# State-space segments from ten-row products of cumulative sums, in a two-block fp32 kernel on one core

## The chip, the cores and the metric

The kernel runs on one core of one Trainium2 chip. The metric is the device time of one execution in microseconds (us), as the median of several; a lower number is better. The engines of the core are named as in the profile: PE is the matrix engine (PEld its weight loads), DVE the vector engine, ACT the scalar engine, POOL the GpSimd engine, SP the engine that issues most transfers.

## The reference

A sequence of 512 tokens of width 1024 goes through a first block (gated convolution, feed-forward, banded attention, feed-forward) and a second block (a state-space mixer, "SSD", then gated linear attention, "GLA"), all in fp32. The part that the change touches is the scan of the SSD mixer, which is run forwards and, on the reversed sequence, backwards; `cum` is the running sum of the negative log decays `lac` within a chunk of 128 tokens:

```
cum = jnp.cumsum(lac, axis=1)
decay = jnp.exp(jnp.where(causal, cum[:, :, None] - cum[:, None], -jnp.inf))
xdt = xc * dtc[..., None]
cb = jnp.einsum('blgn,bsgn->blsg', cc, bc)
y = jnp.einsum('blsgr,bsgrp->blgrp', cb[..., None] * decay, xdt)
y = y + jnp.einsum('blgn,bgrpn->blgrp', cc, state) * jnp.exp(cum)[..., None]
```

`dt` is a softplus of a projection to 2 x 32 heads plus a bias, and `lac = dt * a`. There are 8 groups of 4 heads, and 4 chunks.

## The kernel before

Every engine has its own program, written out by hand in program order; semaphores named with `S(...)` tie them together. Nothing is reordered by a scheduler. The weights come in 168 units of 1 MB: SP loads a unit (`load`), ACT rounds it to `whi` (`high`), POOL makes the rest `wlo` (`low`), and PE computes each product as three matmuls, hi x hi, hi x lo and lo x hi (`product`, L1684 to L1686). The normed input is kept as `hHi`, `hLo` in the fixed part of SBUF. Everything else that a stage needs lies in areas that are laid over one another, behind the fixed tiles; the last fixed tiles are `stat`, `g45` (8 columns of 4 bytes) and the two `t32`. The moving operands of the output projections (`yHi`, `f0aHi`, `f1aHi`, `oHi`, `sHi`, `gHi` and their low parts) are in such areas.

The SSD stage first projects x, B, C and `dt` of group 0, turns `dt` into log decays `la` per token, and makes `ecum`, `wst` and `etot` with 24 small matmuls against triangles of ones (L2010). Then it runs `group(g)` for 8 groups. On PE a group is: `turn_in` (transposes and B C^T), `segments` for 4 chunks, the projections of group g+1 (`project(g + 1, q)`, q = 0 to 3) put between them, `turn_out` of the group before, `increments` of the states, `chunk_out` for 4 chunks, and the two halves of z (`z_half`). The work on a chunk n = 4g + c is:

- ACT builds eight 128x128 pieces `Rm` (mask times a log decay, `segment_rows`, L854), PE multiplies them by GT and LT, forwards and backwards added in one of two PSUM banks (`seg_bank`, L2049, plain fp32), and ACT takes the exponential there (`exponential`, L859);
- POOL makes `coupling(n)`, decay-free weights times dt (`coupled`, L558 and L561), after the six `xw` products and four `ybuf` products of the group;
- DVE multiplies both into `MT` (`mix`, L1430, semaphore `mt_ready`), which `chunk_out` uses (L2097).

On DVE a group also has `taps` (convolution of the next group's projections, L1396 to L1401), `states` (L1439, L1442), `collect` (the output, L1455 to L1459), `masks`, `normalise` and `gate`. In group 0 DVE scales `xT` in eight operations. After the last group, `chan` over 16 tiles of `sHi`, `sLo` starts the output projection.

## Time and profile before

| | us |
|---|---|
| median of 3 runs (2251.29 to 2252.07) | 2251.39 |
| the profiled execution | 2251.21 |
| its span, first to last instruction | 2249.5 |
| PE busy in it | 2154.9 |
| DVE busy | 978.4 |
| POOL busy | 910.0 |
| ACT busy | 828.5 |

The execution lasts 1.7 us longer than its span. A busy engine is one with an instruction in flight; PE is busy in 96% of the span, with a mean granted clock of 0.976 of its full speed, so what is worth time is what PE does, and where it waits.

### The profile page before, as it was taken

The numbers are of one execution on the slowest core, as the hardware profiler recorded it, in microseconds if no ns is written. First come the engines' busy times: TensorE is split into PE (matmuls) and PEld (weight loads), VectorE is DVE, ScalarE is ACT, GpSimd is POOL, SyncE is SP. The second block draws the span as 40 slices with busy tenths as digits, with TensorE's granted clock in tenths as the row PEclk, the third lists the DMA queues.
The fourth block names the chain that finished last, engine by engine and source line by source line (L and its number), as shares of the span: only waits on it lengthen the run. The fifth ranks groups of instructions, "written<-read, shape, count | busy, mean of one in ns | idle before, by whom it ended". The sixth has DMA issues, their size and how long they took to land.

```text
span 2249.5 us, 27332 instructions
## 1 busy us (share of the span) xinstructions
PE 2154.9 (96%) x10885; PEld 1746.7 (78%) x10885; DVE 978.4 (43%) x1435; ACT 828.5 (37%) x1312; POOL 910.0 (40%) x359
## 2 busy tenths in 40 slices
PE   7999999999999989999999999999989989999898
PEld 5877888888777778888888778888868776866676
DVE  3184533323334345343332776766661244452321
ACT  3123222222444332222232555555562154353342
POOL 3434444444322234443441666666654331221232
PEclk9999999999999999999997999999989999999999
DMA  4223333233332123333332211121113321111221
GB/s 135 95 92 104 94 95 111 77 90 101 117 94 76 57 75 94 94 94 94 92 96 63 57 57 57 57 75 57 57 38 94 97 76 38 57 57 38 57 75 57
DMA packets 233244, 176.55 MB, mean 78 GB/s; under 512 B 8483, under 2 KB 229975, under 8 KB 233128
## 3 DMA queue, kind: packets, MB, share of 16 engines
q1 hardware_dynamic: 230460, 174.29, 25.7%
q8 instruction: 84, 1.38, 0.3%
q10 hardware_dynamic: 2668, 0.63, 0.1%
q14 instruction: 32, 0.26, 0.0%
HBM read 172.75 MB, written 2.14 MB: 78 GB/s over the span
## 4 chain that ended last, share of the span: by engine, by line
PE 57%; issue 30%; POOL 8%; DVE 3%; ACT 2%; POOLq 0%; DMA 0%; ACTq 0%; DVEq 0%
PE bank L1684 16%; PE bank L1686 15%; PE bank L1685 15%; POOL wlo L538 7%; PE bank L2049 2%; PE bank L2246 1%; PE bank L2228 1%; PE bank L2097 1%; PE bank L2093 1%; PE bank L2242 1%; PE bank L2063 1%; PE bank L2210 0%; PE bank L2028 0%; PE bank L2254 0%; POOL P L561 0%
## 5 line engine op out<-in xcount | busy, mean ns | idle before, releaser
L538 POOL TENSOR_TENSOR wlo<-raw,whi 128x2048 fp32r<-128x2048 f32 (+1 forms) x168 | 737.9, 4392 | 1236.9 <-ACT whi L616 1236.9
L1684 PE MATMUL bank<-hHi,whi 128*128 128x512 f32 x1408 | 563.1, 400 | 8.0 <-DVE hLo L1156 5.3
L1686 PE MATMUL bank<-hHi,wlo 128*128 128x512 f32 x1408 | 549.9, 391 | 0.0
L1685 PE MATMUL bank<-hLo,whi 128*128 128x512 f32 x1408 | 549.5, 390 | 0.0
L616 ACT ACTIVATE whi<-raw 128x2048 fp32r<-128x2048 f32 (+1 forms) x168 | 303.8, 1809 | 476.0 <-PE bank L1686 474.3
L1684 PEld LDWEIGHTS bank<-hHi,whi 128*128 128x128 f32 x1408 | 265.3, 188 | 73.8 <-issue 13.7
L1685 PEld LDWEIGHTS bank<-hLo,whi 128*128 128x128 f32 x1408 | 265.4, 188 | 59.8 <-issue 5.7
L1686 PEld LDWEIGHTS bank<-hHi,wlo 128*128 128x128 f32 x1408 | 265.1, 188 | 56.3
L1684 PE MATMUL bank<-whi,hHi 128*128 128x256 f32 x896 | 260.2, 290 | 5.9 <-ACT lg L1026 3.9
L1685 PE MATMUL bank<-wlo,hHi 128*128 128x256 f32 x896 | 255.9, 286 | 0.0
L1686 PE MATMUL bank<-whi,hLo 128*128 128x256 f32 x896 | 255.6, 285 | 0.0
L1684 PEld LDWEIGHTS bank<-whi,hHi 128*128 128x128 f32 x896 | 174.2, 194 | 24.6 <-issue 18.7
L1685 PEld LDWEIGHTS bank<-wlo,hHi 128*128 128x128 f32 x896 | 174.3, 195 | 0.4 <-issue 0.2
L1686 PEld LDWEIGHTS bank<-whi,hLo 128*128 128x128 f32 x896 | 174.3, 195 | 0.0
L1188 DVE TENSOR_TENSOR xT<-xT,bank 128x512 f32<-128x512 f32 x48 | 33.0, 687 | 312.2 <-PE bank L1686 312.2
L636 ACT ACTIVATE hHi<-xT,vecT 128x512 fp32r<-128x512 f32 x40 | 28.0, 717 | 127.0 <-DVE xT L1188 127.0
L1156 DVE SCALAR_TENSOR_TENSOR hLo<-xT,vecT,hHi 128x512 fp32r<-128x512 f32 x40 | 61.2, 1544 | 29.7 <-ACT hHi L636 29.7
L1401 DVE SCALAR_TENSOR_TENSOR xc<-bank,vecT,xc 128x510 f32<-128x510 f32 (+1 forms) x96 | 71.9, 749 | 3.4
L1684 PE MATMUL bank<-f0aHi,whi 128*128 128x512 f32 x176 | 69.5, 395 | 0.0
L1684 PE MATMUL bank<-f1aHi,whi 128*128 128x512 f32 x176 | 69.5, 395 | 0.0
L1686 PE MATMUL bank<-f0aHi,wlo 128*128 128x512 f32 x176 | 69.5, 395 | 0.0
L1686 PE MATMUL bank<-f1aHi,wlo 128*128 128x512 f32 x176 | 69.5, 395 | 0.0
(325 smaller groups left out, 3178.8 us busy)
## 6 DMA issues: line engine op xcount, KB each, us to landing
raw<-in_ssd_w_in SPq DMA_DIRECT2D x48, 512.0 KB, 4.6
raw<-in_ffn_w_gate SPq DMA_DIRECT2D x44, 512.0 KB, 4.7
raw<-in_ffn_w_up SPq DMA_DIRECT2D x44, 512.0 KB, 4.7
raw<-in_gla_w_in SPq DMA_DIRECT2D x40, 512.0 KB, 4.7
raw<-in_conv_w_in SPq DMA_DIRECT2D x24, 512.0 KB, 4.4
raw<-in_ffn_w_down SPq DMA_DIRECT2D x32, 384.0 KB, 3.6
raw<-in_attn_w_qkv SPq DMA_DIRECT2D x24, 512.0 KB, 4.7
raw<-in_ffn_w_down SPq DMA_DIRECT2D x32, 320.0 KB, 4.0
```

Of the source, the lines that this page charges most:

```text
L538: pool.tensor_tensor(wlo[s][:, 0:w], raw[s][:, 0:w], whi[s][:, 0:w].bitcast(F32), ALU.subtract).then_inc(w_lo, 1)
L616: act.activation(whi[s][:, 0:w], raw[s][:, 0:w], ACT.Copy).then_inc(w_hi, 1)
L636: act.activation(dst, src, ACT.Copy, scale=scale).then_inc(sem, 1)
L1156: stt3(tile(hLo, k), tile(xT, k), gain(j, k), tile(hHi, k).bitcast(F32), ALU.mult, ALU.subtract).then_inc(h_ready, 1)
L1188: tt(x, x, bank[b][:, :], ALU.add).then_inc(res_done, 1)
L1401: ins = stt3(y[:, to:to + w], u[:, frm:frm + w], tapcol(j, ct), y[:, to:to + w], ALU.mult, ALU.add)
L1684: pe.matmul(dst, hi1, hi2, start=first, stop=False)
L1685: pe.matmul(dst, hi1, lo2, start=False, stop=False)
L1686: return pe.matmul(dst, lo1, hi2, start=False, stop=last)
L2049: ins = pe.matmul(seg_bank(c)[:, :], mat[:, :], rows(n, d), start=(d == 0), stop=(d == 1))
L2063: ins = pe.matmul(bank[4 + step][:, 256 * d:256 * d + 256], bt[:, P * c:P * (c + 1)], xw_buf(step, d), start=True, stop=True)
L2093: pe.matmul(carried_bank(c, d), conv_tile(g, 3)[:, P * c:P * (c + 1)], m["stt"][:, SEQ * step + 256 * d:SEQ * step + 256 * d + 256], start ...
```

## The change

1. **Segments.** The log decays are not multiplied by triangles any more. `dt` is projected with the 64 heads as rows and the 512 tokens as columns (24 matmuls in place of 96), and DVE runs a scan along the tokens for each direction. The cumulative sums go, split into a high and a low part, to DRAM (`cums`), and 12 small transfers a group bring them back as two operands for each direction: `U` and `L`, ten rows for each chunk (two rows of sums or ones, eight of picks). PE then forms `cum - cum` for 4 heads as one product of ten rows in the faster fp32r format, forwards in bank 2 (`FB`) and backwards in bank 3 (`BB`). ACT copies `BB` to `back` (`back_out`), DVE takes the smaller of both (`least`), ACT the exponential, DVE `mix`. The two banks serve every chunk.
2. **ecum, wst, etot** are made in the same layout and turned to tokens by 12 transposes and one small matmul.
3. **Order.** `mix(n)` of a group's first chunk stands ahead of `taps(g + 1, 0)`; `chunk_out(g, 0)` stands ahead of `segments(g, 3)`; both z halves of group 0 and `project(1, 0)` stand ahead of group 0; the scaling of `xT` is spread over seven groups.
4. **The end.** Part of the splits of `sY` stand inside the last group, and the first output tile is computed over 14 tiles, then the last two.
5. **Areas.** `g45` gets 64 columns, so all areas behind it start 224 bytes later, on the same remainder modulo 512 bytes as `hHi`. With 8 columns they started 288 bytes past it.

```diff
-        m_g45 = sb("g45", [P, KT])
+        m_g45 = sb("g45", [P, 64])
...
+                def decay_rows(g):
+                    if g:
+                        sp.wait_ge(S("rows_ready"), 4 * g)
+                    for d in range(2):
...
+                        for r in range(2):
...
+                            sp.dma_start(U[r::32, :].rearrange("c (h e) -> c h e", h=HPG), src).then_inc(S("rows_in"), 16)
+                        for c in range(NT):
...
+                            sp.dma_start(L[32 * c + 2:32 * c + 2 + 2 * HPG, :], src).then_inc(S("rows_in"), 16)
...
-                def segment_rows(n):
...
-                            act.activation(rows(n, d)[:, P * h:P * (h + 1)], mask[:, :], ACT.Copy, scale=m["la"][:, at:at + 1]).then_inc(S("rm_ready"), 1)
+                def rows(g):
+                    act.wait_ge(S("rows_in"), 192 * (g + 1))
+                    for d in range(2):
+                        for name in (f"U{d}", f"L{d}"):
+                            copy(m[name][:, :], m[f"{name[0]}in{d}"][:, :], S("rows_ready"))
+                def back_out(n):
+                    act.wait_ge(S("seg"), n + 1)
+                    if n:
+                        act.wait_ge(S("seg_least"), n)
+                    if n >= NT and n % NT == 0:
+                        act.wait_ge(S("y_squared"), n)
+                    copy(m["back"][:, :], BB[:, :], S("back_ready"))
                 def exponential(n):
-                    act.wait_ge(S("seg"), n + 1)
-                    act.activation(seg_bank(n)[:, :], seg_bank(n)[:, :], ACT.Exp).then_inc(S("ex_ready"), 1)
+                    act.wait_ge(S("seg_least"), n + 1)
+                    act.activation(FB[:, :], FB[:, :], ACT.Exp).then_inc(S("ex_ready"), 1)
...
+                def least(n):
+                    dve.wait_ge(S("back_ready"), n + 1)
+                    tt(FB[:, :], FB[:, :], m["back"][:, :], ALU.min).then_inc(S("seg_least"), 1)
...
+                for d in range(2):
+                    way = slice(None, None, -1 if d else 1)
+                    chain(dve.tensor_tensor_scan(dirs_of(cum)[d][:, way], dirs_of(again)[d], dirs_of(laT)[d][:, way], 0.0, ALU.mult, ALU.add))
...
-                for c in range(NT):
-                    for k in range(KT):
-                        x = slice(SEQ * k + P * c, SEQ * k + P * (c + 1))
-                        w = slice(64 * k, 64 * k + 64)
-                        ins = product(bank[4][:, 64 * c:64 * c + 64], hHi[:, x], hLo[:, x], m["wdtHi"][:, w], m["wdtLo"][:, w], k == 0, k == KT - 1)
+                for k in range(KT):
+                    x, w = slice(SEQ * k, SEQ * (k + 1)), slice(DTH * k, DTH * (k + 1))
+                    ins = product(bank[4][0:DTH, :], m["wdtHi"][:, w], m["wdtLo"][:, w], hHi[:, x], hLo[:, x], k == 0, k == KT - 1)
...
                 def segments(g, c):
                     n = NT * g + c
-                    pe.wait_ge(S("rm_ready"), 8 * n + 8)
-                    if n >= 2:
-                        pe.wait_ge(S("mt_ready"), n - 1)
-                    if g > 1 and c < 2:
-                        pe.wait_ge(S("sz_ready"), NT * g - 2 * c)
-                    for d, mat in enumerate((GT, LT)):
-                        ins = pe.matmul(seg_bank(c)[:, :], mat[:, :], rows(n, d), start=(d == 0), stop=(d == 1))
+                    if c == 0:
+                        pe.wait_ge(S("rows_ready"), 4 * g + 4)
+                        if g > 1:
+                            pe.wait_ge(S("sz_ready"), NT * g)
+                    if n:
+                        pe.wait_ge(S("mt_ready"), n)
+                    at = slice(32 * c, 32 * c + 2 + 2 * HPG)
+                    for d, dst in enumerate((FB, BB)):
+                        ins = pe.matmul(dst[:, :], m[f"L{d}"][at, :], m[f"U{d}"][at, :], start=True, stop=True)
                     ins.then_inc(S("seg"), 1)
...
+                    if k == 0:
+                        pe.wait_ge(S("y_bank_free"), NT * SSD_GROUPS - 1)
+                        mark(chan(bank[0][:, :], 0, lambda k: P * k, sHi, sLo, range(14), True, False, inner_ready="sy_lo"))
```

What stands on DVE in a middle group from `normalise` to the second `mix`, before (`MT` is what `mix` writes; `bank<-bank,rstd` to the last `xc` are one call of `taps`):

```order
L1422 TENSOR_TENSOR szs<-szs,stat 128x1024 [waits dve_chain]
L1396 TENSOR_TENSOR bank<-bank,rstd 128x512 [waits mm]
...
L1401 SCALAR_TENSOR_TENSOR xc<-bank,vecT,xc 128x510 [waits dve_chain]
L1430 TENSOR_TENSOR MT<-bank,P 128x512 [waits y_mm,p_ready,ex_ready]
L1442 COPY stt<-bank 128x512 [waits state_mm,y_mm]
L1439 TENSOR_TENSOR stt<-stt,etot 128x512 [waits state_ready]
...
L1396 TENSOR_TENSOR bank<-bank,rstd 128x512 [waits mm,state_ready]
...
L1430 TENSOR_TENSOR MT<-bank,P 128x512 [waits y_mm,p_ready,ex_ready]
```

And now:

```order
L1513 TENSOR_TENSOR szs<-szs,stat 128x1024 [waits dve_chain]
L1518 TENSOR_TENSOR bank<-bank,back 128x512 [waits back_ready]
L1526 TENSOR_TENSOR MT<-bank,P 128x512 [waits y_mm,p_ready,ex_ready]
L1487 TENSOR_TENSOR bank<-bank,rstd 128x512 [waits mm]
...
L1538 COPY stt<-bank 128x512 [waits state_mm,y_mm]
L1535 TENSOR_TENSOR stt<-stt,etot 128x512 [waits state_ready]
...
L1518 TENSOR_TENSOR bank<-bank,back 128x512 [waits back_ready,state_ready]
L1526 TENSOR_TENSOR MT<-bank,P 128x512 [waits y_mm,p_ready,ex_ready]
L1487 TENSOR_TENSOR bank<-bank,rstd 128x512 [waits mm]
```

The first `mix` has moved ahead of the first `taps`, a `least` (L1518) stands ahead of each `mix`, and the second `mix` stands behind `taps` and `states` and ahead of the second `taps`.

What stands on PE in a middle group from the third chunk's segments (`Rm`) to the first chunk's output (`MT`), before (the 24 matmuls of `project(g + 1, 2)` begin with the row on `whi`):

```order
L2049 MATMUL bank<-Rm,GT 128x512 [waits mt_ready,rm_ready]
L2049 MATMUL bank<-Rm,LT 128x512
L1684 MATMUL bank<-hHi,whi 128x512 [waits tap_done,w_lo]
...
L2049 MATMUL bank<-Rm,GT 128x512 [waits mt_ready,rm_ready]
L2049 MATMUL bank<-Rm,LT 128x512
L2093 MATMUL bank<-stt,xC 128x256 [waits state_ready]
L2097 MATMUL bank<-xt,MT 128x64 [waits mt_ready]
```

And now:

```order
L2178 MATMUL bank<-U,L 128x512 [waits mt_ready]
L2178 MATMUL bank<-U,L 128x512
L1807 MATMUL bank<-hHi,whi 128x512 [waits tap_done,w_lo]
...
L2222 MATMUL bank<-stt,xC 128x256 [waits state_ready]
L2226 MATMUL bank<-xt,MT 128x64 [waits mt_ready]
...
L2178 MATMUL bank<-U,L 128x512 [waits mt_ready]
L2178 MATMUL bank<-U,L 128x512
```

The fourth chunk's segments have moved behind the first chunk's output. The wait on `mt_ready` has the same name, but in the diff above its count has risen from n - 1 to n.

## Rows read from the trace of the kernel before

**Rows 1.** The page: busy time of each engine over the span.

```profile
PE 2154.9 (96%) x10885; PEld 1746.7 (78%) x10885; DVE 978.4 (43%) x1435; ACT 828.5 (37%) x1312; POOL 910.0 (40%) x359
```

**Rows 2.** Stretches group 1, 3: length; busy PE, PEld, DVE, ACT, POOL; PEclk, DMA, GB/s.

```profile
1312.37:1367.15 54.78, 54.78 (x294) 46.02 (x295) 36.11 (x56) 28.87 (x63) 29.34 (x24) 0.95 0.18 53
1419.22:1471.29 52.07, 52.07 (x294) 43.62 (x293) 36.26 (x54) 30.45 (x64) 34.89 (x25) 1.00 0.21 61
```

**Rows 3.** The chain that ended last, in group 3: start us, us, what.

```profile
1421.43 1.72 PE bank L2049 x4
...
1429.05 2.59 PE bank L2063 x12
...
1455.01 0.86 PE bank L2093 x4
1455.87 0.84 PE bank L2097 x8
...
1462.51 0.86 PE bank L2093 x4
```

**Rows 4.** Timeline of DVE, group 3: start us, us, operation [idle before].

```profile
1428.65 0.70 DVE L1396 TENSOR_TENSOR bank<-bank,rstd 128x512 f32<-128x512 f32 x1 [2.87 <-PE bank L1686]
...
1433.19 0.68 DVE L1430 TENSOR_TENSOR MT<-bank,P 128x512 f32<-128x512 f32 x1
1433.79 0.68 DVE L1442 COPY stt<-bank 128x512 f32<-128x512 f32 x1
1434.51 1.91 DVE L1439 TENSOR_TENSOR stt<-stt,etot 128x512 f32<-128x512 f32 x1
...
1437.90 0.69 DVE L1442 TENSOR_TENSOR stt<-stt,bank 128x512 f32<-128x512 f32 x1
...
1451.65 0.41 DVE L1455 TENSOR_TENSOR yt<-bank,ecum 128x256 f32<-128x256 f32 x1
...
1453.01 0.69 DVE L1430 TENSOR_TENSOR MT<-bank,P 128x512 f32<-128x512 f32 x1
```

**Rows 5.** Timeline of POOL, group 3.

```profile
1420.94 2.62 POOL L572 TENSOR_TENSOR t<-xt,wst 128x256 f32<-128x256 f32 x4 [11.28 <-ACT xt L636]
...
1431.28 4.59 POOL L538 TENSOR_TENSOR wlo<-raw,whi 128x2048 fp32r<-128x2048 f32 x1
...
1445.50 1.05 POOL L558 TENSOR_TENSOR P<-dt,CB 128x512 f32<-128x512 f32 x1
...
1449.03 1.04 POOL L558 TENSOR_TENSOR P<-dt,CB 128x512 f32<-128x512 f32 x1
```

**Rows 6.** Timeline of ACT, group 3.

```profile
1425.28 0.58 ACT L859 ACTIVATE bank<-bank 128x512 f32<-128x512 f32 x1
...
1438.93 1.91 ACT L616 ACTIVATE whi<-raw 128x2048 fp32r<-128x2048 f32 x1 [2.60 <-PE bank L1686]
```

**Rows 7.** Timeline of PE behind two gaps: group 0, and group 1's start.

```profile
1292.44 1.10 PE L2049 MATMUL bank<-Rm,GT 128*128 128x512 f32 x2 [2.29 <-DVE MT L1430]
...
1312.37 1.94 PE L2028 MATMUL bank<-ident,xc 128*128 128x128 f32 x8 [4.71 <-DVEq L1457]
```

**Rows 8.** Timeline of PE: the dt projection's first, and the first behind project(0, 1).

```profile
1203.68 0.42 PE L1684 MATMUL bank<-wdtHi,hHi 128*128 128x64 f32 x1 [3.67 <-DVE wdtLo L1361]
...
1231.87 1.02 PE L1727 MATMUL bank<-acc,ones 128*128 128x512 f32 x2
```

**Rows 9.** Groups of instructions by line: the reversed scan of the GLA stage.

```profile
L1564 DVE TENSOR_TENSOR_SCAN kg<-acc,lg 128x512 f32<-128x512 f32 x4 | 9.3, 2326 | 0.0
```

**Rows 10.** One line's instructions on f0aHi: min/median/max ns, first and last start.

```profile
L1684 PE MATMUL bank<-f0aHi,whi x176: 393/396/399, 447.2 to 569.7; 128*128 128x512 f32 x176
```

**Rows 11.** Timeline of PE in the last projection: hHi as moving operand.

```profile
2163.34 0.39 PE L1686 MATMUL bank<-hHi,wlo 128*128 128x512 f32 x1
...
2166.08 0.39 PE L1686 MATMUL bank<-hHi,wlo 128*128 128x512 f32 x1
```

**Rows 12.** Timeline of PE: the first matmul of the SSD output projection.

```profile
1668.08 0.76 PE L1684 MATMUL bank<-sHi,whi 128*128 128x512 f32 x1 [10.44 <-DVE sLo L1470]
```

More of the change, by code:

```diff
@@ L497, in _ @@
                     load(U_SSD + n, n % 2, src)
+                    if n == 1:
+                        picks()
+                    elif n == 3:
+                        cums_out()
+                        decay_rows(0)
+                    elif kind == "bc" and g:
+                        decay_rows(g)
                 pairs(U_SSD_OUT, 4, lambda i, s: cols(A["ssd_w_out_2"][0], 256 * i + P * s, P))
@@ L875, in squares @@
                             act.wait_ge(S("y_squared"), NT * g + c)
-                        act.activation(m["ysq"][:, :], chunk("szs", c), ACT.Square, accum_out=stat[:, NT * g + c:NT * g + c + 1]).then_inc(S("y_squared"), 1)
+                        act.activation(m["back"][:, 0:256], chunk("szs", c), ACT.Square, accum_out=stat[:, NT * g + c:NT * g + c + 1]).then_inc(S("y_squared"), 1)
                 def group_root(g):
@@ L906, in group @@
                         group_root(g - 1)
+                    back_out(NT * g)
                     exponential(NT * g)
-                    segment_rows(NT * g + 2)
+                    if not more:
+                        act.wait_ge(S("cb_mm"), SSD_GROUPS)
+                        for k in range(3):
+                            y_hi(k)
                     if g != 1:
@@ L912, in group @@
                         turned_out(g - 1, 0)
+                    back_out(NT * g + 1)
                     exponential(NT * g + 1)
-                    segment_rows(NT * g + 3)
+                    if not more:
+                        act.wait_ge(S("rows_ready"), 4 * SSD_GROUPS)
+                        for k in range(3, 5):
+                            y_hi(k)
                     if more:
@@ L935, in group @@
                     else:
-                        for k in range(7):
+                        ahead(U_SSD_OUT, 0, 0)
+                        for k in range(5, 8):
                             y_hi(k)
@@ L1477, in group @@
                         normalise(g - 1)
-                    else:
-                        dve.wait_ge(S("r4_ready"), 1)
-                        for k in range(KT):
-                            x = tile(xT, k)
-                            stt3(x, x, col("final_norm", k), m["yt"][:, :], ALU.mult, ALU.mult).then_inc(res_done, 1)
-                        dve.wait_ge(res_done, 8 * (R_MID + 1))
+                    least(n)
+                    mix(n)
                     if more:
                         taps(g + 1, 0)
-                    mix(n)
                     states(g)
-                    if more:
-                        taps(g + 1, 1)
-                    mix(n + 1)
+                    least(n + 1)
+                    if more and g == 0:
+                        taps(1, 1)
+                    mix(n + 1)
+                    if more and g:
+                        taps(g + 1, 1)
+                    elif not more:
+                        for k in range(3):
+                            y_low(k)
+                    least(n + 2)
+                    collect(g, 0)
+                    mix(n + 2)
+                    if not more:
+                        for k in range(3, 5):
+                            y_low(k)
                     if more:
                         taps(g + 1, 2)
-                    mix(n + 2)
-                    collect(g, 0)
-                    mix(n + 3)
+                    least(n + 3)
                     if more:
                         taps(g + 1, 3)
+                    mix(n + 3)
                     collect(g, 1)
@@ L2105, in group @@
                     segments(g, 0)
-                    if more:
+                    if not more:
+                        z_half(g, 0)
+                    elif g:
                         project(g + 1, 0)
-                    else:
-                        z_half(g, 0)
                     if g:
@@ L2122, in group @@
                         project(g + 1, 2)
+                    chunk_out(g, 0)
                     segments(g, 3)
-                    chunk_out(g, 0)
                     if more:
@@ L2133, in group @@
                     chunk_out(g, 3)
+                project(1, 0)
+                pe.wait_ge(S("decay_kept"), 5)
                 for g in range(SSD_GROUPS):
@@ L2143, in _ @@
                         pe.wait_ge(res_done, 8 * R_SSD + k - 1)
[L2144 to L2150 removed]
+                    if k == 0:
+                        pe.wait_ge(S("y_bank_free"), NT * SSD_GROUPS - 1)
+                        mark(chan(bank[0][:, :], 0, lambda k: P * k, sHi, sLo, range(14), True, False, inner_ready="sy_lo"))
+                        pe.wait_ge(S("y_bank_free"), NT * SSD_GROUPS)
+                        for e in range(2):
+                            turn_out(LAST_G, e)
+                        mark(chan(bank[0][:, :], 0, lambda k: P * k, sHi, sLo, range(14, IT), False, True, inner_ready="sy_lo"))
+                        continue
+                    for half in range(2):
+                        mark(chan(bank[k % 2][:, :], k % 2, lambda k: P * k, sHi, sLo, range(8 * half, 8 * half + 8), half == 0, half == 1))
             if on("gla"):
```

229 lines of the change are left out of this document (143 added, 86 removed).

## The prediction

> **What bounds the kernel now.** I read the page first: PE is busy 2154.9 us of the span [rows 1], so work taken from PE, or a wait put on it, decides. Then the stretches of the SSD stage: groups 2 to 6 each last 52.07 us with PE busy in all of it at full clock, while DVE, ACT and POOL are busy 36.3, 30.5 and 34.9 us [rows 2]. So PE alone sets the group's length, and the others have slack in sum. The chain that ended last gives what a group is made of [rows 3], and the timelines of the other three engines give where their work lies inside it [rows 4 to 6]. That matters because the change ties PE to them more tightly.
>
> **Part 1: what PE no longer does in a group.** The two segment matmuls of a chunk take 1.72 us in fp32 [rows 3]. In fp32r a matmul of 512 columns takes 0.23 us (12 steps in 2.74 us) [rows 11], so the pair takes 0.46. No row has an fp32r matmul of ten rows: its bounds are 0.46 and, if it gained nothing, 1.72. I take 0.46, since the rows of that format have the same 512 columns. Four chunks save 5.0 us: 47.0 us of PE work a group.
>
> **Part 2: what PE now waits for.** Before, `segments(n)` waited for `mix` of chunk n - 2, so the ACT, POOL and DVE work of a chunk lay beside a projection. Now one pair of banks serves all chunks, and it waits for `mix(n - 1)`. The loop is PE, ACT copy, DVE `least`, ACT exponential, DVE `mix`, PE. I lay a group 3 on one axis, T = 0 at its start (1419.22) [rows 2].
>
> - PE: `turn_in` ends at 1421.43, T + 2.2. `project` with `turn_out` takes 1429.05 - 1423.15 = 5.9 us (5.5 alone, 24 x 0.228), the increments 2.6, `chunk_out` 1.70 (1.27 for the first and last), half a z 1462.51 - 1456.71 = 5.8 [rows 3, 11].
> - First wait. POOL starts at 1420.94 and does xw, ybuf and `coupled` until it takes up wlo at 1431.28, T + 12.1 [rows 5]; the change leaves that work alone. `mix` takes 0.68 [rows 4], so `segments(g, 1)` starts at T + 12.9. PE is free at 2.2 + 0.46 + 5.9 + 2.6 = 11.2. Gap 1.7 us. Before, this wait had no effect, since the second chunk's segments did not need it.
> - Second wait. Behind `mix(0)` (begun at 12.1, 0.6 until the next) DVE does `taps` (1433.19 - 1428.65 = 4.5 us) and `states` (1433.79 to 1438.59, less a stall of 1.2 us, = 3.6) [rows 4]: 20.8. `least` costs as `mix` 0.7, the exponential 0.6 [rows 6], `mix` 0.7, hand-overs 0.3: `mt_ready` at 23.1. PE has done segments, project and turn_out at 12.9 + 0.5 + 5.9 = 19.3. Gap 3.8 us.
> - Third wait. PE: 23.1 + 0.5 + 5.5 + 1.3 (`chunk_out(g, 0)`) = 30.3. Now DVE has `collect` ahead of the third `mix`: 1453.01 - 1451.65 = 1.4 us [rows 4]; and POOL's `coupled(2)` ends at 22.2 (second exponential) + 1.9 (high) + 4.6 (wlo) + 3.5 (1445.50 to 1449.03) = 32.2 [rows 5, 6]. `mix` ends at 32.9. Gap 2.6 us.
> - Behind it nothing waits: 32.9 + 0.5 + 5.5 + 1.7 + 5.8 + 1.7 + 5.8 + 1.3 = 55.1 us. The fourth `mix` ends near T + 44.5 (two more `taps` on DVE), before `z_half(g, 1)` asks for it at 48.
>
> So a middle group takes 55.1 us at full clock, in place of 52.07: 5.0 us of work saved, 8.1 us of gaps made. ACT loses 32 mask products a group and gains eight copies; DVE gains four `least` (2.8 us) and one `xT` scaling. These fit in their slack, and cost only where they stand in the chain, as counted. The 12 row transfers of a group are issued a group ahead of their use, with the next weight unit behind them on SP's queue; the queue waits there for POOL most of the time, and that unit is wanted about half a group later. If that cover went, ACT's `high` of that unit would be late, then wlo and the next `coupled`.
>
> **Part 3: the clock behind gaps.** A gap of 4.71 us stands ahead of group 1, and one of 2.29 us inside group 0 [rows 7]; both times the matmuls behind it run longer for some microseconds, the 2 records of the former taking 1.10. Group 1 has the same 294 matmuls as group 3, no gap inside, a granted clock of 0.95 and 54.78 us [rows 2]: the half clock (1.2 GHz) after the gap costs 2.7 us. In the changed group the slow stretch behind the first gap is swallowed by the second gap; behind the second and third it is not. Bounds: 0 and 2 x 2.7 = 5.4. I take 2.4, near the middle: both gaps of rows 7 show the slow stretch, but part of one can fall into the wait behind it. A group: 57.5 us. Groups 1 to 6 last 54.78 + 5 x 52.07 = 315.1 now, and 345 then: **+30 us** (bounds +16 and +48).
>
> The Trainium skill, page "TensorE: Matmul & The Clock Gate", section "HAM oscillation — how this bites in real kernels", has the same: recurring waits inside a loop put the array back to half rate each time. By that alone each group would pay the upper bound.
>
> **Part 4: the start.** From the first dt matmul to the end of `project(0, 1)` PE takes 28.2 us [rows 8]. With 24 + 24 matmuls it takes 11.0, and 2 more at half clock, since the 3.67 us gap ahead stays: -15 us. But the new chain is longer: copy, bias, softplus on ACT, `taps(0, 0)`, then on DVE two scans of 2.3 and half as much [rows 9] and six more operations of 0.7, and only then the other `taps`; `project(1, 0)` has to wait for the third. Group 0 starts some 8 us earlier. In it nothing covers the waits, as `project(1, 0)` is used up: 12.9 us to `segments(0, 1)` with PE idle for over half, 4.5 + 3.6 + 0.7 + 4.5 + 0.7 until the next `mix`, and then as above. All-SBUF operations of DVE can stretch while POOL works (the `states` product takes 1.91 in place of 0.69 beside wlo) [rows 4, 5]. Group 1 then starts at about 1310.7 in place of 1312.37: **-1.7 us**, bounds -6 and +4. Most of the 15 us is given back.
>
> **Part 5: the end.** The first output tile now has work in the 10.44 us hole [rows 12]: 14 tiles are 42 matmuls, 9.8 us. But the chunk chain of the last group ends some 4 us later by the same steps, `y_low` beyond the fifth still lie behind it on DVE, and tiles 14 and 15 need the same `normalise`. **-3 us**, bounds -7 and +2.
>
> **Part 6: the areas.** The output projections read their moving operand from areas. 525 steps on `f0aHi` take 569.7 - 447.2 = 122.5 us, 0.2333 us each [rows 10]; on `hHi` in the same kind of loop 0.2283 [rows 11]. By the sizes in the code the areas lie 32 bytes off a multiple of 64, `hHi` on one; then they agree. yHi 192, f0aHi 528, f1aHi 528, oHi 192, sHi 384 and gHi 192 matmuls, 2016 in all, times 5.0 ns: **-10 us**. Bounds 0 (another cause) and -13.
>
> The same page, section "Wait — 56ns, not 53.3ns?", gives a warm matmul of 512 columns a fixed 215.7 ns whatever its address; by it this edit would give nothing. The two rows differ from each other and from it, so I keep the rows.
>
> **Sum.** Against the profiled execution, 2251.2 us, 0.2 under the median: 2251.2 + 30 - 1.7 - 3 - 10 = **2266.5**, forecast 2266.
>
> **Rivals.**
> - *The gaps come, the clock stays.* A group of 55.1: 2251.2 + 15.5 - 14.7 = 2252. For it: slow stretches that fall into the waits; against: both gaps of rows 7. Chance 0.14.
> - *PE stays the bound, faster.* If POOL's `coupled` and DVE's order delivered `mix` before PE asks, a group is 47.0 and the total 2251.2 - 33 - 14.7 = 2203; part of it (51 us a group) gives 2227. For it: all engines but PE have a third of their time free [rows 2]. Against: the first wait hangs on POOL's unchanged 12.1 us, the second on DVE's fixed order. It decides from a group under 54.2 us. Chance 0.20, most of it in the partial form.
> - *The areas give nothing*: the 5 ns a step between rows 10 and 11 come from something else than the address, and stay: 2276. Chance 0.14. That is how it would come out by the page's figure in part 6.
> - The forecast: 0.52, its own range 2254 to 2279.
>
> **How the numbers follow.** A measurement here tells 0.2% (4.5 us) from no change. Slower: the forecast, the third rival: 0.64 after a share for a start or end better than I think. Same: most of the first, 0.14. Faster: 0.22. The range 2236 to 2284 leaves out the full form of the second rival and the upper bounds falling together.
>
> **What would show it.** PE rows on the U,L pair at 0.23 us each; groups 1 to 6 of 55 to 59 us, with three gaps a group before the segments, released by `MT`, of about 2, 4 and 2.5 us; granted clock under 1 in each group; `f0aHi` steps at 0.228; POOL's first wlo of a group still at T + 12. I am wrong if groups are at 52 or less, if the second gap is missing because DVE gets to `least` sooner, or if the `f0aHi` steps stay at 0.233.

## The result

The changed kernel takes 2293.84 us (median of 4 runs, 2291.21 to 2295.6) and the kernel before, on the same chip, 2251.73 us (2251.29 to 2252.49). The ratio is 1.0185, with a 95% interval of 1.0171 to 1.0198: slower by 42 us. The forecast had the direction right and the size wrong: 2266, and the time lies above the range, which ended at 2284. The profiled execution has a span of 2293.8 us, 44.3 more than the 2249.5 of before.

The page's busy line, to be read against [rows 1]: PE is busy 15.6 us less, and its share of the span falls from 96% to 93%, so it waits more. DVE is busy 38 us more and ACT 44 less.

```profile
PE 2139.3 (93%) x10715; PEld 1739.9 (76%) x10715; DVE 1016.5 (44%) x1473; ACT 784.6 (34%) x1126; POOL 910.1 (40%) x371
```

The stretches from one `turn_in` to the next, groups 1 to 6 (columns as in [rows 2]):

```profile
1304.43:1365.15 60.72, 54.15 (x284) 46.15 (x285) 41.95 (x61) 22.95 (x39) 29.75 (x24) 0.91 0.17 49
1365.15:1427.05 61.90, 54.63 (x286) 45.98 (x286) 40.36 (x59) 24.56 (x40) 34.80 (x25) 0.89 0.18 52
1427.05:1488.77 61.72, 54.48 (x287) 45.88 (x286) 40.49 (x59) 24.56 (x40) 34.80 (x25) 0.89 0.18 53
1488.77:1547.03 58.26, 51.83 (x286) 44.02 (x286) 42.13 (x59) 24.44 (x40) 34.98 (x25) 0.94 0.19 56
1547.03:1610.75 63.72, 56.64 (x286) 47.31 (x286) 39.70 (x59) 24.55 (x40) 34.74 (x25) 0.87 0.18 51
1610.75:1672.72 61.97, 54.75 (x286) 45.99 (x286) 40.29 (x59) 24.55 (x40) 34.80 (x25) 0.89 0.18 52
sum 368.29, PE 326.47 PEld 275.34 DVE 244.92 ACT 145.61 POOL 203.86; mean PE 54.41 PEld 45.89 DVE 40.82 ACT 24.27 POOL 33.98
```

A group lasts 61.4 us in the mean, where groups 2 to 6 lasted 52.07. The six add 53 us, more than the whole loss. PE is both idle (61.72 - 54.48 = 7.2 us in group 3) and slow (granted clock 0.89). In the timeline of PE for group 3, all three gaps that the prediction listed are there, with their releaser:

```profile
1429.36 0.73 PE L2178 MATMUL bank<-U,L 10*128 10x512 f32 x2
...
1430.35 0.40 PE L1808 MATMUL bank<-hLo,whi 128*128 128x512 f32 x1
...
1440.66 0.73 PE L2178 MATMUL bank<-U,L 10*128 10x512 f32 x2 [1.90 <-DVE MT L1526]
...
1442.74 0.63 PE L1808 MATMUL bank<-hLo,whi 128*128 128x512 f32 x1
1443.17 0.63 PE L1809 MATMUL bank<-hHi,wlo 128*128 128x512 f32 x1
...
1448.51 0.60 PE L2204 MATMUL bank<-ident,szs 128*128 128x128 f32 x4
...
1451.44 0.73 PE L2178 MATMUL bank<-U,L 10*128 10x512 f32 x2 [2.33 <-DVE MT L1526]
...
1459.29 0.60 PE L2222 MATMUL bank<-stt,xC 128*128 128x256 f32 x2
...
1463.74 1.22 PE L2178 MATMUL bank<-U,L 10*128 10x512 f32 x2 [3.01 <-DVE MT L1526]
...
1472.48 1.03 PE L2222 MATMUL bank<-stt,xC 128*128 128x256 f32 x4
```

Read the starts against each other. From the second pair to `turn_out` (1440.66 to 1448.51) is 7.85 us, from the third to `chunk_out(g, 0)` 7.85 again, from the fourth to `chunk_out(g, 1)` 8.74. A pair and a projection take 6.25 us at full clock (shown below, where the gaps are filled). So each of the three gaps, the one of 1.90 us too, has matmuls at half clock behind it (a step of 0.43 us, 1442.74 to 1443.17, where full clock has 0.23), which cost 1.6, 1.6 and 2.5 us.

Outside the SSD groups, the output projections' steps are shorter, and the first dt matmul comes 7.9 us sooner than in [rows 8]. These are the line of the page for `f0aHi` (389 ns a record against 396 in [rows 10]) and PE's timeline at the dt projection and at group 1's start:

```profile
L1807 PE MATMUL bank<-f0aHi,whi 128*128 128x512 f32 x176 | 68.5, 389 | 0.0
```

```profile
1195.76 0.69 PE L1807 MATMUL bank<-hHi,wdtHi 128*64 128x512 f32 x1 [4.29 <-DVE wdtLo L1455]
...
1304.43 1.94 PE L2153 MATMUL bank<-ident,xc 128*128 128x128 f32 x8 [3.53 <-DVEq L1553]
```

From there to group 1 is 108.67 us, and was 1312.37 - 1203.68 = 108.69 before.

### The profile page after: what moved, and what is told of

It reads as the page before. It is cut to its first block, busy times and chain, and to the rows that moved or that the text cites. A ratio compares the mean times of both kernels' runs of the same rounds, so it can differ in the third digit from the quotient of the medians.

```text
span 2293.8 us, 26980 instructions
## 1 busy us (share of the span) xinstructions
PE 2139.3 (93%) x10715; PEld 1739.9 (76%) x10715; DVE 1016.5 (44%) x1473; ACT 784.6 (34%) x1126; POOL 910.1 (40%) x371
## 4 chain that ended last, share of the span: by engine, by line
PE 49%; issue 30%; POOL 9%; DVE 8%; ACT 2%; DMA 0%; POOLq 0%; ACTq 0%; DVEq 0%
PE bank L1807 14%; PE bank L1808 14%; PE bank L1809 14%; POOL wlo L603 7%; PE bank L2380 1%; DVE xc L1492 1%; PE bank L2362 1%; PE bank L2226 1%; POOL t L637 1%; PE bank L2222 1%; DVE MT L1526 1%; PE bank L2376 1%; DVE ybuf L1555 1%; PE bank L2178 1%; DVE stt L1538 1%
## 5 line engine op out<-in xcount | busy, mean ns | idle before, releaser
L1807 PE MATMUL bank<-hHi,whi 128*128 128x512 f32 x1408 | 573.2, 407 | 13.3 <-DVE hLo L1250 7.0
L1808 PE MATMUL bank<-hLo,whi 128*128 128x512 f32 x1408 | 563.8, 400 | 0.0
L1809 PE MATMUL bank<-hHi,wlo 128*128 128x512 f32 x1408 | 563.4, 400 | 0.0
L1807 PEld LDWEIGHTS bank<-hHi,whi 128*128 128x128 f32 x1408 | 274.6, 195 | 89.3 <-issue 26.0
L1808 PEld LDWEIGHTS bank<-hLo,whi 128*128 128x128 f32 x1408 | 274.7, 195 | 58.1 <-issue 1.2
L1809 PEld LDWEIGHTS bank<-hHi,wlo 128*128 128x128 f32 x1408 | 273.7, 194 | 59.2
L2178 PE MATMUL bank<-U,L 10*128 10x512 f32 x64 | 27.6, 516 | 61.6 <-DVE MT L1526 61.6
L1808 PE MATMUL bank<-f0aLo,whi 128*128 128x512 f32 x176 | 68.5, 389 | 0.0
```

The source lines that it names most:

```text
L1807: pe.matmul(dst, hi1, hi2, start=first, stop=False)
L1808: pe.matmul(dst, hi1, lo2, start=False, stop=False)
L1809: return pe.matmul(dst, lo1, hi2, start=False, stop=last)
L2178: ins = pe.matmul(dst[:, :], m[f"L{d}"][at, :], m[f"U{d}"][at, :], start=True, stop=True)
```

## The experiments

Each expectation names its own theory A and its rival B. From the filled gaps on, A is mostly this: the 53 us are the waits of PE on the single pair of banks, as DVE's order spaces them, and the half clock behind each wait. B is that something else makes the group long, above all slower POOL and DVE operations, the added copy and `least`, or the ten-row matmuls themselves. "Middle groups" are groups 2 to 5.

### Areas back, and areas alone

```diff
-        m_g45 = sb("g45", [P, 64])
+        m_g45 = sb("g45", [P, KT])
```

> The changed kernel with the small buffer g45 at its former width of 8 columns, so that every later buffer moves back by the 32 bytes of the change (per partition 224 bytes fewer); nothing else. Theory A (the place of the moving operand sets the step of an fp32r matmul): the steps on f0aHi go back from 0.227 to 0.2333 us and 2016 matmuls cost some 12 us, so the time is 2293.8 + 12 = about 2306 (2302 to 2310). Rival B (the steps shortened for another reason, such as another mix of transfers): 2294 within 3 us, steps unchanged.

> The kernel before with g45 made 64 columns wide, the areas part of the change alone. Theory A: the f0aHi steps fall from 0.2333 to 0.227 and the time from 2251.7 to about 2240 (2237 to 2243), middle SSD groups stay at 52.07. Rival B (the gain needs the rest of the change): 2251 to 2252.

The first took 2308.01 us (2300.24 to 2311.68), 14 more than the changed kernel; the second (the opposite edit on the kernel before, with `tt(m_g45[:, 0:KT], ...)`) 2237.77, ratio 0.9939 (0.9922 to 0.9955). One line's instructions on `f0aHi` in the two kernels, first the areas back, then the areas alone:

```profile
L1807 PE MATMUL bank<-f0aHi,whi x176: 393/396/399, 448.3 to 570.8; 128*128 128x512 f32 x176
```

```profile
L1684 PE MATMUL bank<-f0aHi,whi x176: 389/389/389, 447.6 to 566.6; 128*128 128x512 f32 x176
```

The 525 steps take 122.5 us with the areas back and 119.0 with them moved: 0.2333 and 0.2267 us each. The place of the moving operand is the cause, alone and in both kernels (the weights `whi` and `wlo` are allocated ahead of `g45` and do not move); the part is worth 13 to 14 us, and needs nothing of the rest. Only two places were tried, 288 bytes past the remainder of `hHi` modulo 512 bytes and on it, so the runs don't say which multiple of bytes counts. In this version (areas alone) the stretch from group 7 to the end is 617.83 us, and was 622.18; with the whole change it is 621.08, so the change at the end, the areas apart, costs 3.25 us where the prediction had a gain of 3.

### Gaps filled

```diff
+                    if c and g < LAST_G:
+                        pe.wait_ge(S("back_ready"), n)
+                        for _ in range((0, 7, 9, 12)[c]):
+                            pe.matmul(BB[:, :], hHi[:, 0:P], hHi[:, 0:SEQ], start=True, stop=True)
                     if n:
                         pe.wait_ge(S("mt_ready"), n)
```

> The changed kernel with matmuls that compute nothing in the three gaps of groups 0 to 6: 7, 9 and 12 fp32r matmuls of 128x128 by 128x512 (1.6, 2.1 and 2.7 us at full clock) into the second segment bank, once its copy is taken and before the wait for mix. The waits on mix stay as they are. Theory A (the waits cost 7 us a group and the half clock behind them another 4 to 7): PE stays at full clock, a middle group goes from 61.4 to 55 to 57 us, the time from 2294 to 2255 to 2270, although PE does more work. Rival B (the matmuls behind the gaps are long for another reason, such as the port that DVE and POOL share, or the gaps themselves are all of it): group stays at 60 to 62, time 2290 to 2300.

2280.14 us (2277.58 to 2281.7), ratio 1.0127 (1.011 to 1.0144): 13.7 us less than the changed kernel, for 28 more matmuls a group. Neither range held it. In groups 4 and 5 the clock stayed at 1.00 and a group lasted 57.4 us; in groups 2, 3 and 6 it was 0.97 even so, and they lasted 59.0 to 59.3. The stretches of groups 3 and 4, and in the timeline of PE the three later pairs of group 4, with what follows two of them:

```profile
1420.41:1479.39 58.98, 56.79 (x315) 47.89 (x314) 41.53 (x59) 24.45 (x40) 35.06 (x25) 0.97 0.19 55
1479.39:1536.82 57.43, 55.23 (x314) 46.85 (x314) 42.19 (x59) 24.46 (x40) 34.87 (x25) 1.00 0.20 57
```

```profile
1493.04 0.73 PE L2182 MATMUL bank<-U,L 10*128 10x512 f32 x2 [0.33 <-DVE MT L1526]
...
1499.30 0.60 PE L2208 MATMUL bank<-ident,szs 128*128 128x128 f32 x4
...
1503.86 0.74 PE L2182 MATMUL bank<-U,L 10*128 10x512 f32 x2 [1.88 <-DVE MT L1526]
...
1514.30 0.73 PE L2182 MATMUL bank<-U,L 10*128 10x512 f32 x2
...
1520.53 1.03 PE L2226 MATMUL bank<-stt,xC 128*128 128x256 f32 x4
```

This run parts clock from waits. At a granted clock of 1.00 the same waits make a group of 57.4 us; with the clock that the changed kernel gets, 61.4. So 4.0 us a group are the clock and the rest are waits. Two small things hide in that figure and nearly cancel: the twelve matmuls of the third gap outlast its wait by 0.3 us (`mix` is done by 1514.0, the pair starts at 1514.30), and the `collect` ahead of that `mix` takes 0.5 us less here than in the changed kernel. The matmuls were filling: of 55.23 busy us, 28 x 0.228 = 6.4 are theirs, which leaves 48.8 us of PE's own work in a group. A pair and a projection take 1499.30 - 1493.04 = 6.26 us, and 1520.53 - 1514.30 = 6.23. The axis of the prediction can be laid over it: the three pairs start at T + 13.65, 24.5 and 34.9, where it had 12.9, 23.1 and 32.9.

### PE's and DVE's order

All three keep the work of the changed kernel. On PE, `segments(g, c)` moves behind the projection that followed it; on DVE, `taps(g + 1, 0)` moves ahead of `mix(n)`, and `mix(n + 3)` ahead of `taps(g + 1, 3)`. PE's edit, then DVE's:

```diff
-                    segments(g, 1)
                     if more:
                         project(g + 1, 1)
+                    segments(g, 1)
...
-                    segments(g, 2)
                     if more:
                         project(g + 1, 2)
+                    segments(g, 2)
                     chunk_out(g, 0)
-                    segments(g, 3)
                     if more:
                         project(g + 1, 3)
+                    segments(g, 3)
```

```diff
-                    mix(n)
                     if more:
                         taps(g + 1, 0)
+                    mix(n)
...
+                    mix(n + 3)
                     if more:
                         taps(g + 1, 3)
-                    mix(n + 3)
```

> The changed kernel in another order, same work: on PE segments(g,1) stands behind project(g+1,1), segments(g,2) behind project(g+1,2) with chunk_out(g,0) next, segments(g,3) behind project(g+1,3); on DVE taps(g+1,0) stands ahead of mix(n) and mix(n+3) ahead of taps(g+1,3). Laid out on the axis of the prediction, mix is then done before PE asks for it: segments 1 to 3 asked for at T+17, 23 and 31, mix done at about T+13.5, 20 and 27. Theory A (the loss of a group is its waits on the single pair of banks, and the clock behind them): no gap, full clock, a middle group 47 to 49 us, time 2293.8 - 6 x 13 = about 2213 (2205 to 2225). Rival B (POOL and DVE are slowed by the shared port or bound by their sums, or the ten-row matmuls cost more than their records show): group 52 or more, time 2240 or more.

> The changed kernel with DVE's order alone altered: taps(g+1,0) ahead of mix(n), mix(n+3) ahead of taps(g+1,3); PE's order as changed. Theory A (the second gap is DVE's order: mix, taps, states, least in a row): the states end 4.5 us sooner, the second gap goes, gaps 1 and 3 of about 2 us stay, a middle group 51 us at full clock and 53 to 55 with the clock, time 2240 to 2262. Rival B (the order of one engine alone moves nothing, the wait only passes to PE's next request): 2280 or more.

> The changed kernel with PE's order alone altered: each segments(g,c) of c above 0 behind the projection that followed it, chunk_out(g,0) behind segments(g,2); DVE's order as changed. Theory A: segments ask a projection later, the gaps ahead of them shrink to about 1 us in all, and DVE's late taps(g+1,1) hold project(g+1,3) for 2.6 us instead; a middle group 51 to 53 us, time 2230 to 2250. Rival B (DVE's chain stays the bound whatever PE asks first): gaps of 7 us a group remain in another place, time 2280 or more.

The times in us, with the ratio to the kernel before and its interval:

| | DVE as changed | DVE reordered |
|---|---|---|
| PE as changed | 2293.84 (1.0185, 1.0171 to 1.0198) | 2278.64 (1.0128, 1.0111 to 1.0144) |
| PE reordered | 2243.36 (0.997, 0.9959 to 0.9981) | 2235.03 (0.9926, 0.9909 to 0.9942) |

With DVE's order alone the second gap goes, as theory A said, but gaps of 2.3 and 3.0 us stay and the granted clock is 0.91 to 0.94: middle groups of 57.2 to 58.5, not 53 to 55. The time fell into neither range (2240 to 2262, or 2280 and more): PE's work of 48.8, gaps of 5.3 and some 4 us of clock make 58, where theory A had 51 at full clock. With PE's order alone the time is in theory A's range, though a group is 54.6 and not 51 to 53. The row of a middle group:

```profile
1401.67:1456.23 54.56, 51.71 (x287) 43.79 (x286) 41.67 (x59) 24.33 (x40) 34.97 (x25) 0.94 0.21 60
```

The timeline of PE has the waits at the predicted places, 0.5 us ahead of a segment pair (some 1 expected) and 2.3 (2.6 expected) ahead of `project(g + 1, 3)`, released by the taps:

```profile
1426.16 0.73 PE L2178 MATMUL bank<-U,L 10*128 10x512 f32 x2 [0.51 <-DVE MT L1526]
1430.69 0.79 PE L1807 MATMUL bank<-hHi,whi 128*128 128x512 f32 x1 [2.33 <-DVE xc L1492]
```

With both, none is left ahead of a segment pair in groups 1 to 6. The time still missed the 2205 to 2225 of theory A, because a group is 52.1 to 53.7 and not 47 to 49. Rival B had named 52 or more, with 2240 or more; the time lies between the two. PE's own work is 48.8, and two other waits show, one on the second taps and one of `z_half(g, 0)` on the last `least`:

```profile
1428.37 0.50 PE L1807 MATMUL bank<-hHi,whi 128*128 128x512 f32 x1 [0.99 <-DVE xc L1492]
1438.98 0.36 PE L1807 MATMUL bank<-whi,hHi 128*128 128x256 f32 x1 [2.32 <-DVE bank L1518]
```

### The last least ahead of the third taps

To the version with both orders:

```diff
+                    least(n + 3)
                     if more:
                         taps(g + 1, 2)
-                    least(n + 3)
                     mix(n + 3)
```

> The version with the segments one projection later (2235.0), and least(n+3) ahead of taps(g+1,2) on DVE. There z_half(g,0) waited 2.3 us for least(n+3), which stood behind those taps. Theory A: that wait goes, DVE waits 1.8 us instead at a place where nothing hangs on it, a middle group 49.5 to 50.5 us in place of 52.2 to 53.7, time 2217 (2213 to 2222). Rival B (chunk_out(g,2) or the next turn_in then waits for the later taps): 2230 to 2236.

2218.34 us (2217.07 to 2220.48), ratio 0.9859 (0.9843 to 0.9875): theory A, and the fastest here that computes the whole result, 1.4% faster than before with every part of the change in it. A middle group, and its one remaining gap in the timeline of PE:

```profile
1445.58:1495.40 49.82, 48.74 (x287) 41.66 (x286) 41.38 (x60) 24.44 (x41) 35.66 (x25) 1.00 0.22 65
```

```profile
1472.70 0.50 PE L1807 MATMUL bank<-hHi,whi 128*128 128x512 f32 x1 [1.08 <-DVE xc L1492]
```

Groups 2 to 5 are all like this; group 6, with the same wait, had a clock of 0.97 and lasted 51.4. The same copies, `least`, ten-row pairs and single pair of banks take 49.8 us a group here and 61.4 in the changed kernel. So the added work does not by itself make a group slow.

### Forward direction alone: two banks and one

```diff
-                    for d, dst in enumerate((FB, BB)):
-                        ins = pe.matmul(dst[:, :], m[f"L{d}"][at, :], m[f"U{d}"][at, :], start=True, stop=True)
-                    ins.then_inc(S("seg"), 1)
+                    pe.matmul(seg_bank(c)[:, :], m["L0"][at, :], m["U0"][at, :], start=True, stop=True).then_inc(S("seg"), 1)
```

> The changed kernel, and of the segments the forward direction alone, in two banks in turn, each waiting for mix(n-2) as in the kernel before. It leaves out the backward segment matmul, the ACT copy back and DVE's least; the exponential has a factor of 0.01 in it, so that its values stay finite. Theory A (the single pair of banks makes the gaps): no gap ahead of segments, only project(g+1,3) waits some 2.5 us for taps(g+1,1); a middle group 47 to 50 us, time 2205 to 2230. Rival B (the gaps come from the slower coupled and states): 2260 or more. To be read beside the next run.

> As the run before it, with the same work left out, but with one bank for all four chunks, so that each segment matmul waits for mix of the chunk just before. Theory A (the single bank is the cause, the copy and least only lengthen its loop by 1.4 us): gaps of about 1.9, 2.2 and 2.1 us and the clock behind them, a middle group 55 to 59 us, time 2258 to 2280. Rival B (the copy and least are the cause): as fast as with two banks, 2205 to 2230.

> The run with the forward direction alone in two banks (2253.7), and DVE's order of the run with the vector order alone: taps(g+1,0) ahead of mix(n), mix(n+3) ahead of taps(g+1,3). The same work is left out: backward segment matmul, copy, least, and a factor of 0.01 in the exponential. There z_half(g,0) waited 3.7 to 5.1 us for mix(n+3) and project(g+1,3) 1.8 for the taps. Theory A (the gaps are DVE's order against PE's; with two banks and this order neither side waits): a middle group 46 to 49 us, time 2190 to 2215. Rival B (another wait of 4 us or more turns up behind it): 2235 or more.

These three leave out the backward direction, so their results are not those of the reference. Two banks took 2253.72 us (ratio 1.0011, 1.0001 to 1.0021), one bank 2272.29 (1.0094, 1.0077 to 1.0111), two banks with DVE's other order 2212.01 (0.9827, 0.981 to 0.9843). One bank was as expected: three gaps of 2.1, 1.2 and 2.2 us in middle groups and 58.0 us, without copy and `least`. It also prices the added work under the changed order: without it a middle group is 3.4 us shorter than the 61.4 of the changed kernel. Two banks fell between theory A's 2205 to 2230 and rival B's 2260. No segment matmul waits in middle groups, but the wait turns up elsewhere, in PE's timeline of group 3:

```profile
1434.58 0.53 PE L1803 MATMUL bank<-hHi,whi 128*128 128x512 f32 x1 [1.85 <-DVE xc L1489]
1447.19 0.55 PE L1803 MATMUL bank<-whi,hHi 128*128 128x256 f32 x1 [5.11 <-DVE MT L1522]
```

`z_half(g, 0)` needs the bank of the fourth chunk, whose `mix` the changed DVE order puts behind the fourth taps: 56.3 to 57.5 us a group. So my sentence "no gap ahead of segments" held, and its conclusion did not: I had looked at one user of the bank. Of the 18.6 us between one bank and two, 12.2 lie in group 0 (its turn_in to the next, 55.13 against 42.88); in a middle group the second bank is worth only 0.5 to 1.7 us as long as both orders stay as changed. With DVE's other order (the third of these runs) a group is 50.4 to 50.6; the time is in theory A's range, the group above its 46 to 49. Under this DVE order and the changed PE order, two banks make a group of 50.5 us and the single pair one of 58.0 (the run with DVE's order alone; it has backward matmul, copy and `least` besides).

### Two that did not help

The first is an edit of the fastest version, with the last `least` early; its core, for the last group:

```diff
+                    if not more:
+                        for k in range(3):
+                            y_low(k)
                     mix(n)
```

> The fastest version so far (2218.3), in group 0 with taps(1,0) behind mix(0) again, where chunk_out(0,2) waited 4.0 us for the third taps, and in the last group with the first three y_low between least and mix of the first chunk, where DVE idled 5.0 us, the next two behind the last mix, and collect(g,0) behind the third mix, so that least and mix of the third chunk no longer stand behind 4.2 us of y_low and 1.4 of collect. Theory A: 1 to 2 us less in group 0, the 3.5 us wait ahead of the fourth segments falls under 1, time 2213 to 2216. Rival B (both stretches end with another wait, for POOL or the normalisation): 2217 to 2220.

2224.27 us (2222.0 to 2228.53): 6 slower than the version that it starts from, and neither range. Group 0 went from 48.20 to 52.03: with `mix(0)` ahead of the taps again, PE waited 3.80 us for taps and 1.81 for a `mix` where it had waited 2.89 once, and the 4.04 us wait of `chunk_out(0, 2)` stayed; in the last group the second pair's wait grew from 2.18 to 3.39 and the fourth's from 3.49 to 4.44.

The second edit puts this in the changed kernel's group 0, between `least(0)` and `mix(0)`, and takes the scaling away from the ends of the groups:

```diff
+                        for k in range(KT):
+                            x = tile(xT, k)
+                            stt3(x, x, col("final_norm", k), m["r4"][:, :], ALU.mult, ALU.mult).then_inc(res_done, 1)
```

> The changed kernel with the eight scalings of xT (1.1 us each) all in group 0, between least and mix of its first chunk, as the kernel before had them in that group, instead of one at each group's end beside POOL's xw. Same work. Theory A (the scaling lies on the port that DVE and POOL share and stretches xw from 3.8 to 5.3 us, so that coupled(0) ends at T+12.7 in place of 12.1): xw goes back to 3.8, the first segments wait ends 0.6 to 1.5 us sooner, groups 1 to 6 are 60 to 61 us in place of 61.4, and group 0 pays 1 to 3 us. Time 2288 to 2294. Rival B (xw is stretched by DVE's szs product and collect alone): xw stays above 5 us, groups as they were, time 2294 to 2298.

2298.09 us (2296.89 to 2298.64). POOL's first operations of a group in the changed kernel, and then here (timelines):

```profile
1428.94 3.06 POOL L637 TENSOR_TENSOR t<-xt,wst 128x256 f32<-128x256 f32 x4 [10.18 <-ACT xt L705]
1431.97 2.24 POOL L637 TENSOR_TENSOR xw<-xt,wst 128x256 f32<-128x256 f32 x2
...
1439.79 4.55 POOL L603 TENSOR_TENSOR wlo<-raw,whi 128x2048 fp32r<-128x2048 f32 x1
```

```profile
1430.62 2.62 POOL L637 TENSOR_TENSOR t<-xt,wst 128x256 f32<-128x256 f32 x4 [10.13 <-ACT xt L705]
1433.21 1.18 POOL L637 TENSOR_TENSOR xw<-xt,wst 128x256 f32<-128x256 f32 x2
...
1440.96 4.57 POOL L603 TENSOR_TENSOR wlo<-raw,whi 128x2048 fp32r<-128x2048 f32 x1
```

`xw` goes from 5.3 to 3.8 us as theory A had it, wlo starts at T + 12.2 in place of 12.7, and the first gap is 1.39 in place of 1.90. The half microsecond is kept down the chain. Group 3 as a stretch, and its last pair in the timeline of PE:

```profile
1428.74:1490.16 61.42, 54.68 (x286) 46.00 (x286) 39.58 (x58) 24.56 (x40) 34.30 (x25) 0.89 0.18 53
```

```profile
1464.91 1.22 PE L2178 MATMUL bank<-U,L 10*128 10x512 f32 x2 [3.00 <-DVE MT L1526]
```

That pair starts at T + 36.2, and did at T + 36.7; the group lasts 61.4 us, and lasted 61.7. Groups 2 and 6, which had a clock of 0.89 in both traces, are 0.5 and 0.6 shorter as well. The sum of groups 1 to 6 is nevertheless the same, 368.37 us against 368.29, since group 4 of the changed kernel had a clock of 0.94 and lasted 58.26, while here no group got more than 0.89. The time is on the edge of rival B's range, but B's reason is refuted: group 0 grew from 58.03 to 61.46, and the clock of single groups, which the edit does not steer, took back the rest.

## Why the prediction was wrong

The step that failed is the term of groups 1 to 6: forecast +30 us with an upper bound of +48, measured +53.6 against the kernel with the areas alone. The waits and the clock that make it up were both foreseen, and both were sized too small: the axis of the waits by 2.0 to 2.3 us a group, 12 to 14 in all, and the half clock by 1.6 to 1.9, 10 to 11 in all (which of each depends on the 0.3 us by which the filling matmuls outlast the third wait).

The spans differ by 44.3 us. Against the run with the areas alone (span 2236.2) the parts can be read one by one:

| term | predicted | measured |
|---|---|---|
| areas | -10 | -13.3 |
| start, to group 1 | -1.7 | +0.75 (1304.43 against 1303.68) |
| groups 1 to 6 | +30 | +53.6 (368.29 against 314.69) |
| end | -3 | +3.25 |

**Part 6, areas: right, a little small.** 6.7 ns a step and not 5.0, since the steps fell to 0.2267 and not to the 0.2283 of [rows 11].

**Part 2, three waits: the mechanism right, the axis 2 us short.** All three gaps are at their places, released by `MT`. At full clock a group is 57.4 where "55.1 us at full clock" stood. First, T = 0 was set 0.16 us late: `turn_in` of group 3 began at 1419.06 and not at 1419.22, as the timeline of PE in the kernel before has it,

```profile
1419.06 1.04 PE L2028 MATMUL bank<-ident,xc 128*128 128x128 f32 x8
```

and all my places are counted from here. Then the pair behind the first wait is 0.6 late. Nearly all of that is POOL, whose 12.1 (12.2 from the true start) I had taken as unchanged, and which the moved `xT` scaling stretched to 12.7; the last run, with the scaling elsewhere, gave 12.2 again. The next is another 0.6 late: the states' products took 1.11 and 0.94 us for the 0.69 I had, while POOL worked. In DVE's timeline of group 3:

```profile
1445.78 1.11 DVE L1535 TENSOR_TENSOR stt<-stt,etot 128x512 f32<-128x512 f32 x1
...
1447.64 0.94 DVE L1535 TENSOR_TENSOR stt<-stt,etot 128x512 f32<-128x512 f32 x1
...
1450.69 0.69 DVE L1526 TENSOR_TENSOR MT<-bank,P 128x512 f32<-128x512 f32 x1 [0.65 <-ACT bank L943]
...
1460.76 0.42 DVE L1551 TENSOR_TENSOR yt<-bank,ecum 128x256 f32<-128x256 f32 x1 [4.24 <-PE bank L2226]
...
1461.67 1.29 DVE L1555 TENSOR_TENSOR ybuf<-ybuf,yt 128x256 f32<-128x256 f32 x1 [0.16 <-DVE ybuf L1552]
1462.99 0.69 DVE L1526 TENSOR_TENSOR MT<-bank,P 128x512 f32<-128x512 f32 x1
```

The rows from 1460.76 to 1462.99 are `collect`, which takes 2.2 us where I had 1.4 (1.7 with the gaps filled). The third `mix` stands right behind it. I had let POOL's `coupled(2)` end this wait; POOL was done with it at 1460.5, in its timeline

```profile
1459.24 1.26 POOL L626 TENSOR_TENSOR P<-P,acc 128x512 f32<-128x512 f32 x1
```

so what ends the third wait is a loop through PE itself: `chunk_out(g, 0)`, then `collect`, then `mix`. That is why the slow stretch behind the second wait is not swallowed by the third.

**Part 1, the pair: too cheap.** It costs 1430.35 - 1429.36 less one step of 0.23, that is 0.76 us, and not 0.46; by the same reading the old pair is 1.72. PE's work in a group fell from 52.07 to 48.8, by 3.3 us where the text had 5.0; the four pairs are 1.2 of these 1.7, and the other 0.5 was not traced. Where a wait ends the stretch this is hidden; it counts ahead of the last wait and behind it, 0.3 each. The filling matmuls' own 0.3 and 0.1 of small terms make the rest of the 2.3. It also means that rival two's 47 us was never to be had.

**Part 3, the clock: too cheap.** The text said that the slow stretch behind the first gap is swallowed by the second and that the others are not, and then took 2.4 us "near the middle" of 0 and 5.4. Its own mechanism, priced by the rows, is the 1.6 and 2.5 us behind the second and third wait, 4.1 in all, and the filled gaps show 4.0. Its 2.4 is 1.6 less than that, and with the 2.3 of the waits this is the 3.9 a group, 23 us in six groups, by which Part 3's 57.5 fell short of 61.4. A middle value between bounds was the wrong choice where the mechanism itself named which of the stretches count.

The Trainium skill, "TensorE: Matmul & The Clock Gate", section "HAM oscillation — how this bites in real kernels", has recurring waits that put the array back to half rate each time. In the changed kernel the trace agrees (three waits, granted clock 0.89), though one of the three slow stretches costs no time. The waits of the page's example are for DMA and longer than these, so what waits of 1.9 to 3.0 us do is told by the rows here alone. In the fastest version the one wait of 1.08 us a group leaves the clock at 1.00 in groups 2 to 5, and at 0.97 in group 6.

**Parts 4 and 5.** The start came out 2.5 us worse than forecast and inside its bounds: "most of the 15 us is given back" held, in the gaps of group 0 (5.28, 5.32, 2.15 and 3.53 us). The end was outside by 1.25: the bound +2 against +3.25. The last group has waits of 2.06, 4.77 and then 3.96 us ahead of the output projection; I had counted its chunk chain as 4 us longer and the work for the hole as worth more. No run took the end apart from the rest, so how its 3.25 us divide stays open.

**Rivals.** The first (the clock stays) is refuted by the clock rows, the second by three gaps a group, the third by the two area runs. The forecast's case came true, beyond its own range.

## What to carry to other kernels

When a change makes a buffer single, list every instruction that asks for it, and write both orders on one axis: here the 53 us were mostly not the added work but where PE asked and in what order DVE answered, and asking one projection later on PE, with three moves in DVE's order, turned 2294 us into 2218. The added work did cost something while PE waited at the end of the chain (3.4 us a middle group), and with the better orders a group is shorter than before even so. A wait on TensorE should be priced as the idle time plus the half clock behind it, for every wait whose slow stretch does not end in another wait. A gain of half a microsecond a group should be read from groups with the same granted clock: in one trace of the changed kernel the middle groups, all with the same work, last from 58.26 us (clock 0.94) to 63.72 (0.87).

## What the runs showed that I had not expected

- The start address of the moving operand changes the step of an fp32r matmul of 512 columns: 0.2333 us with the areas in their old place, 0.2267 in the new one, 224 bytes later, over 525 steps, in both kernels. The Trainium skill, "TensorE: Matmul & The Clock Gate", section "Wait — 56ns, not 53.3ns?", gives a warm matmul of 512 columns 215.7 ns with no regard to the address; both rows stand above it, and they differ by 3%.
- Gaps alike in size did not have like clocks behind them. The version with both orders had waits of 0.9 to 1.0 and 2.3 us in every middle group, and a granted clock of 1.00 in some and 0.97 in others; PE's order alone, with 0.5 and 2.3 us, had 0.94; filled gaps left 0.33 and 1.88 us, at 1.00 in two groups and 0.97 in three. What parts these is not settled by the runs.
- A pair of ten-row fp32r matmuls costs 0.76 us, and two steps of 128 rows 0.46, though each has 512 columns. With two banks and one matmul a chunk the timeline of PE has

```profile
1475.87 0.49 PE L2173 MATMUL bank<-U,L 10*128 10x512 f32 x1
...
1476.62 0.40 PE L1804 MATMUL bank<-hLo,whi 128*128 128x512 f32 x1
```

  By the same reading a single one costs 1476.62 - 1475.87 - 0.23 = 0.52 us. So the second matmul of a pair adds one step of 0.23, and the 0.3 are paid once for each place in which such matmuls stand between others; why, the runs don't show.
